# Attention and everything behind it in one stage, with the first output-projection tiles between the last heads' blocks

## What is computed

```python
for i in range(2):
    h = rms_norm(x, g[0])
    # layer 0: 16 heads of 64, each query sees a window of 8 x 16 positions
    # layer 1: 8 heads, softmax(q1 k1) - lam * softmax(q2 k2), an rms norm per head
    m = neighborhood_attention(...) if i == 0 else diff_attention(...)   # ends in o @ w_o
    x = x + rms_norm(m, g[1])
    f = conv_glu_ffn(rms_norm(x, g[2]), ...)          # d_ff 2816, conv of width 3, gelu, gate
    x = x + rms_norm(f, g[3])
    gate = sigmoid(rms_norm(x, g[4]) @ ple_w_gate[i])
    x = x + gate * (p[i] @ ple_w_proj[i])
```

## Time and profile before

| what | value |
|---|---|
| median of three runs | 2300.37 us |
| the profiled execution | 2302.38 us |
| its span, first to last instruction | 2300.6 us |
| PE busy (matmul) | 2188.8 us, 95% |
| PEld busy (weight load) | 1737.0 us, 76% |
| DVE busy | 1282.2 us, 56% |
| ACT busy | 903.2 us, 39% |
| POOL busy | 119.6 us, 5% |
| mean granted TensorE clock | 0.983 |

### The profile page before, as it was taken

How to read it: one execution, slowest core, us unless ns; L and a number is a source line. 1 busy time by engine, 2 the same in 40 slices (tenths; PEclk the granted TensorE clock), 3 DMA queues, 4 the chain that set the end, 5 groups by cost and what they waited for, 6 DMA issues and landing times. The chain is left out here.

```text
span 2300.6 us, 35634 instructions
## 1 busy us (share of the span) xinstructions
PE 2188.8 (95%) x14030; PEld 1737.0 (76%) x14030; DVE 1282.2 (56%) x1653; ACT 903.2 (39%) x1415; POOL 119.6 (5%) x96
## 2 busy tenths in 40 slices
PE   9998999999998999899999998999887799999999
PEld 6786788888876677578888876777767656888887
DVE  6554476563376776457565347685435476433333
ACT  5444432222254565543222244654221354322322
POOL 0000011110000000001111000000313100000000
PEclk9999999999999999999999999999988999999999
DMA  6230323333322221223323331322000011333331
GB/s 245 95 127 23 106 92 100 98 93 101 92 73 91 87 64 45 65 73 110 100 91 100 94 96 56 100 83 64 3 3 3 28 47 50 106 100 93 98 99 65
DMA packets 52933, 187.65 MB, mean 82 GB/s; under 512 B 5840, under 2 KB 6096, under 8 KB 52688
## 3 DMA queue, kind: packets, MB, share of 16 engines
q1 hardware_dynamic: 52528, 185.39, 26.2%
q10 hardware_dynamic: 288, 0.59, 0.1%
HBM read 183.86 MB, written 2.10 MB: 81 GB/s over the span
## 5 line engine op out<-in xcount | busy, mean ns | idle before, releaser
L289 PE MATMUL tail_banks<-tail_r_hi,tail_w_hi 128*128 128x512 f32 x1344 | 529.9, 394 | 7.7 <-DVE tail_r_lo L1678 7.4
L291 PE MATMUL tail_banks<-tail_r_hi,tail_w_lo 128*128 128x512 f32 x1344 | 523.2, 389 | 0.0
L290 PE MATMUL tail_banks<-tail_r_lo,tail_w_hi 128*128 128x512 f32 x1344 | 523.1, 389 | 0.0
L289 PEld LDWEIGHTS tail_banks<-tail_r_hi,tail_w_hi 128*128 128x128 f32 x1344 | 252.3, 188 | 68.2 <-DVE tail_r_lo L1678 7.6
L290 PEld LDWEIGHTS tail_banks<-tail_r_lo,tail_w_hi 128*128 128x128 f32 x1344 | 252.3, 188 | 54.5 <-issue 3.3
L291 PEld LDWEIGHTS tail_banks<-tail_r_hi,tail_w_lo 128*128 128x128 f32 x1344 | 252.2, 188 | 52.9
L274 DVE TENSOR_TENSOR tail_w_lo<-ring,tail_w_hi 128x1024 fp32r<-128x1024 f32 x168 | 241.3, 1438 | 90.8 <-ACT tail_w_hi L268 87.5
L268 ACT ACTIVATE tail_w_hi<-ring 128x1024 fp32r<-128x1024 f32 x168 | 176.7, 1056 | 228.4 <-PE tail_banks L291 225.8
L289 PE MATMUL ff_banks<-ff_r_hi,ff_w_hi 128*128 128x512 f32 x512 | 200.0, 391 | 0.0
L290 PE MATMUL ff_banks<-ff_r_lo,ff_w_hi 128*128 128x512 f32 x512 | 199.2, 389 | 0.0
L291 PE MATMUL ff_banks<-ff_r_hi,ff_w_lo 128*128 128x512 f32 x512 | 199.2, 389 | 0.0
(11 more groups left out here) (527 smaller groups left out, 3486.9 us busy)
## 6 DMA issues: line engine op xcount, KB each, us to landing
ring<-weights SPq DMA_DIRECT2D x315, 512.0 KB, 3.6
na_bias<-window_bias SPq DMA_DIRECT2D x16, 512.0 KB, 5.4
da_rel<-t_rel SPq DMA_DIRECT2D x8, 448.0 KB, 4.3
X<-xT SPq DMA_DIRECT2D x8, 256.0 KB, 5.7
outT<-X SPq DMA_DIRECT2D x8, 256.0 KB, 2.1
const<-consts SPq DMA_DIRECT2D x1, 1312.0 KB, 11.3
tail_pt<-pT SPq DMA_DIRECT2D x2, 512.0 KB, 3.5
kr<-mla_consts SPq DMA_DIRECT2D x1, 512.5 KB, 6.0
```

The source lines that it names most:

```text
L289: pe.matmul(psum, hi, self.r_hi[:, rhs_slot, :], start=start, stop=False)
L290: pe.matmul(psum, hi, self.r_lo[:, rhs_slot, :], start=False, stop=False)
L291: return pe.matmul(psum, lo, self.r_hi[:, rhs_slot, :], start=False, stop=stop)
```

## The change

One stage now holds a layer's attention and its tail (`layer`). `neighborhood` and `differential` no longer open a stage: they return four functions, which the engines' programs of the layer call first. The attention's PSUM tiles are now slices of the layer's 8 banks, its softmax buffer `e` lies in `k.H`. Heads don't go to `k.H`: ScalarE writes each head's tile rounded to a slot of `r_hi`, and VectorE its lo part to `r_lo` (`heads_lo`; in layer 1 over a buffer `heads`, `round_head` and `heads_lo`). `weigh` of layer 0 waits for the lo part of the pair before, not for the copy. In layer 1 `head_out` waits for the lo part of the head two before. The q, k, v products read their right side from slots 2 and 3 and six more, so that heads and inputs don't share slots. Chunks 24 to 27 (the projection's first four) are rounded and split in the last chunks' turns. The projection's tiles 0 to 2 are cut into parts by heads (`wo_part(tile, first, end)`) and stand between the last attention steps; in layer 1 three blocks of tile 3 as well. `keep_busy`, the barrier between the two stages, the rounding of the heads in one go and one load of an activation table on ScalarE are gone. The embedding's load is now the first DMA of a layer.

```diff
 def neighborhood(k, st, sp_, banks, sb, rhs, out):
...
         def weigh(t):
             pe.wait_ge(t_free, turn_of(t, 3))
-            pe.wait_ge(o_out, t) if t else pe.wait_ge(rstd_done, 1)
+            pe.wait_ge(out_split, t) if t else pe.wait_ge(rstd_done, 1)
...
+        def wo_part(tile, first, end):
+            if first == 0:
+                pe.wait_ge(evacuated, N - 2 + tile)
+            if tile == 0:
+                pe.wait_ge(out_split, end)
+            wo(pe, tile, first, end)
+
         chunk((2, last), middle=lambda: scores(last, 1))
         turn_weights(last - 1, 1)
+        wo_part(0, 0, 3)
         turn_values(last - 1)
+        wo_part(1, 0, 3)
         weigh(last - 1)
+        wo_part(0, 3, 6)
         turn_weights(last, 0)
+        wo_part(1, 3, 6)
         turn_weights(last, 1)
+        wo_part(2, 0, 3)
         turn_values(last)
+        wo_part(2, 3, 6)
         weigh(last)
+        for tile in range(FIRST):
+            wo_part(tile, 6, 7)
+        for tile in range(FIRST):
+            wo_part(tile, 7, 8)
...
         def split(c):
-            if c < N:
-                sp_.split_chunk(dve, 0, c)
+            sp_.split_chunk(dve, 0, c)
...
+        def heads_lo(t):
+            dve.wait_ge(o_out, t + 1)
+            dve.tensor_tensor(by_block(sp_.lo(out[t])), o_ps.rearrange("p b (r c) -> p b r c", c=QC),
+                              by_block(sp_.hi(out[t])).bitcast(F32), ALU.subtract).then_inc(out_split, 1)
...
         for t in range(PAIRS):
             evacuate((0, t))
+            if t >= 3:
+                heads_lo(t - 3)
...
         maxima(last)
+        heads_lo(last - 2)
         evacuate((2, last))
         normalise(last)
+        heads_lo(last - 1)
+        heads_lo(last)
...
         last = PAIRS - 1
+        round_ahead((2, last))
         weights_out(last - 1, 1)
...
 def differential(k, st, sp_, banks, sb, rhs, out):
...
+        WO_PARTS = {31: (0, 0, 3), 32: (1, 0, 3), 33: (2, 0, 3), 34: (0, 3, 5), 35: (1, 3, 5), 36: (2, 3, 5)}
         for n in range(NBLK + LAG_O):
...
             if n == NBLK - 1:
                 blocks(done, DT * N)
+            if n in WO_PARTS:
+                wo_part(*WO_PARTS[n])
             if 0 <= n - LAG_T < NBLK:
                 turn_weights(n - LAG_T)
...
+        for tile in range(FIRST):
+            wo_part(tile, 5, 6)
         sum_squares(DA_HEADS - 1)
+        for tile in range(FIRST):
+            wo_part(tile, 6, 7)
+        pe.wait_ge(added, NBLK)
+        wo(pe, FIRST, 0, 3)
+        for tile in range(FIRST):
+            wo_part(tile, 7, 8)
...
+            if n >= 15 and n % TT == 3:
+                heads_lo((n - 15) // TT)
         for h in range((NBLK - 13) // TT + 1, DA_HEADS):
             norm(h)
+            heads_lo(h)
...
             if h >= 2:
                 act.wait_ge(summed, h - 1)
-            act.activation(out[:, h, :], o_ps[:, :], ACT.Copy).then_inc(o_out, 1)
+                act.wait_ge(out_split, h - 1)
+            act.activation(heads[:, h % 2, :], o_ps, ACT.Copy).then_inc(o_out, 1)
...
+        def round_head(h):
+            act.wait_ge(normed, h + 1)
+            act.activation(sp_.hi(out[h]), heads[:, h % 2, :], ACT.Copy).then_inc(out_rounded, 1)
...
+            if n >= 14 and n % TT == 2:
+                round_head((n - 14) // TT)
+        round_head(DA_HEADS - 2)
         rsqrt(DA_HEADS - 1)
+        round_head(DA_HEADS - 1)
...
-def layer_tail(k, layer, m):
+def layer(k, layer):
...
             @block.sync
             def _(sp):
                 sp.dma_start(pt[:, :, :], ...).then_inc(s["pt_loaded"], 16)
-                k.refill(sp, N)
+                att.sync(sp)
+                k.refill(sp, N - WO, WO)
...
-                keep_busy(pe, k, banks[:, 3, :], 4)
-                for j in range(DT):
-                    wo_tile(j)
+                att.tensor(pe, wo)
+                wo(pe, FIRST, 3 if layer else 0, DT)
+                for j in range(FIRST + 1, DT):
+                    wo(pe, j, 0, DT)
...
-                sp_.round_chunk(act, 0, 0)
-                for j in range(DT):
-                    sp_.round_rhs(act, k.H[:, j, :], j)
-                for c in (1, 2, 3):
-                    sp_.round_chunk(act, 0, c)
-                act.preload_act_table_set(LN_EXP)
+                att.scalar(act)
```

More of the change, by code:

```diff
@@ new lines, in neighborhood, with slot, half, by_block @@
+    warm_set = st.sem("warm_set")
+    g0 = k.g
+    def slot(t, h):
+        return 2 * (t % 2) + h
+    def half(h):
+        return slice(64 * h, 64 * h + 64)
+    def by_block(x):
+        return x.rearrange("p (r b c) -> p b r c", b=NB, c=QC)
+    def window(x, b):
+        return x.rearrange("p (r c) -> p r c", c=GRID_W)[:, :, KEY_BASE[b]:KEY_BASE[b] + KC]
+    def turn_of(t, kind):
+        return 3 * t + kind
+    def sync(sp):
+        def load_bias(t):
+            if t >= 2:
+                sp.wait_ge(added, 4 * (t - 1))
+            for h in range(2):
+                sp.dma_start(bias[:, slot(t, h), :, :],
+                             k.dram["window_bias"][2 * t + h].rearrange("p (b j) -> p b j", b=NB)).then_inc(bias_loaded[slot(t, h)], 16)
+        load_start(k, sp)
+        sp.dma_start(k.const[:, :], k.dram["consts"]).then_inc(k.const_loaded, 16)
+        load_bias(0)
+        load_bias(1)
+        for c in range(N):
+            sp.wait_ge(k.chunk_split, g0 + c + 1)
+            sp.dma_start(k.ring[:, (g0 + c) % RING, :], k.dram["weights"][g0 + c + RING, :, :]).then_inc(
+                k.ring_full[(g0 + c) % RING], 16)
+            if c >= 7 and c % 3 == 1:
+                load_bias(c // 3)
@@ L1395, in layer_tail @@
-def layer_tail(k, layer, m):
-    WO, PA, UP, DOWN, PB, GATE = 0, DT, DT + 1, DT + 1 + 2 * FT, DT + 1 + 3 * FT, DT + 2 + 3 * FT
-    N = GATE + DT
-    with Stage(k, f"tail{layer}") as st:
+    qb, kb, vb = (sb(n, [P, 2, S]) for n in ("qb", "kb", "vb"))
+    vt = sb("vt", [P, TT, P])
+    rel = sb("rel", [P, 2, W])
+    lam = sb("lam", [P, 4, 64])
+    lprod = sb("lprod", [P, 2, 64])
+    lsum, lexp, nlam = (sb(n, [P, 2]) for n in ("lsum", "lexp", "nlam"))
+    subg = sb("subg", [P, 1])
+    e = k.H[:, 0:4, :].rearrange("p (n m) s -> p n m s", m=2)
@@ L1511, in down @@
                             pe.wait_ge(s["bank_free"], 2 * FT + o - 3)
[L1512 removed]
+                        mm = sp_.multiply(pe, out(o), DOWN + c, o, two[c % 2], start, stop)
                         if stop and o < DT - 1:
```

1195 lines of the change are left out of this document (579 added, 616 removed).

## The result

The changed kernel takes 2275.95 us (median of four runs, 2272.94 to 2279.24) against 2300.43 us (four runs): ratio 0.9895, 95% interval 0.9878 to 0.9913, a gain of 24.5 us. The forecast was 2269.7, with a range of 2264 to 2276. The result lies at the range's slow edge and 6.3 us above the forecast.

The account below looks back on a forecast made before the run. TensorE's own work plus its holes bounds the kernel. Gains of 16.0 us per layer less 1.3 for the embedding's load make 30.7 us, taken off 2300.37: 2269.7 us, range 2264 to 2276.

Parts of the forecast that it names:

- The ends of attention: From the last chunk or blocks into the projection, in both layers: filled holes on PE gain 16.0 us in each.
- the 1.1 us ahead of the first weigh: Layer 0's end: PE waits 1.1 us at pair 6's weigh for a copy on ScalarE, delayed by rounding.
- the 72 matmuls' stretch: Layer 0, first turn after the last chunk to the projection's 73rd matmul: 42.3 us before, 26.3 forecast.
- The new wait in layer 1: Block 31's scores wait 1.3 us for block 30's bias, delayed by chunk 27's rounding and split.
- The other entries of the sum: Layer 1's end without the new wait: scores, turns, products, sums of squares, 81 matmuls and run entries, 34.3 us.
- The thin margins: Layer 1's end: PE reaches the turns of blocks 29 to 31 only 0.3 to 0.5 us after their maps are mixed.
- The start: The embedding's load, now first, delays the first rounding and first matmul by 1.3 us; bounds 0.5 and 2.
- The clock: Both ends of attention: the clock stays at 1.00, as in the pair loop, despite turns mixed with matmuls.
- hidden at no cost: Lo parts inside both layers' loops: subtractions on DVE and layer 1's roundings are covered and cost 0 us.
- the loops: Layer 0's pair loop and layer 1's block loop: forecast to change by 0 us.
- Rival 1: Thin margins fail or loops pay for new DVE and ACT work: 3 to 8 us, 2273 to 2278; chance 0.17.

Follow-up runs that it names:

- the second set: The unchanged code of the changed kernel measured again, against the kernel before: 2272.15 us against 2302.12, ratio 0.9869.

## Why the prediction was right, and where it failed

*The ends of attention.* Right: 16.1 and 16.7 us for 16.0 and 16.0. The step lengths (turn 0.84, weigh 1.97, nine matmuls 2.0) held, the 1.1 us ahead of the first weigh came as 1.09, and of the 72 matmuls' stretch 26.2 us were measured for 26.3. `heads_lo`, taken as 0.7 us from other rows, took 0.68.

*The new wait in layer 1.* Right in place and cause, 1.67 us for 1.3. Block 30's bias started 3.0 us behind its scores (911.96 to 914.97) where I had 2.5, since ScalarE came to the rounding 0.4 us later than I had it. The other entries of the sum were over-counted by 1.1 us, so that the stretch took 34.9 us for 35.6. The thin margins behind it held: no turn waited for DVE.

*The start.* Right: 0.9 to 1.2 us for 1.3.

*The clock.* Right: 1.00 in both mixed stretches, with 153 matmuls between transposes and weighs. The Trainium skill's page "TensorE: Matmul & The Clock Gate", "Part 4: PE-mode transpose", says that transposes don't count as work for the clock. In the changed kernel nothing fell where they were mixed with matmuls; whether they count by themselves no run here shows. What I had not thought of is that the clock can fall behind the wait that I forecast. It did so in two of the kernels measured, behind 1.87 and 1.88 us, and that cost 1.6 us more; in others it stayed up behind 1.67 and 1.78 us. The 2.19 us wait of the kernel before, behind which it stayed up as well, shows that this is no limit to plan by.

*The step that failed* is "hidden at no cost", and in it the loops. I looked there for work on DVE and ACT and found cover for it, rightly. I took over the 0.227 us of one matmul for all matmuls, also for those that now read another buffer, and so put the loops at nothing. It was 0.2333 for 18 of 24, which cost 2.2 us in layer 0 and 1.4 of the 1.6 us in layer 1. Rival 1 had a price for loops that pay, with the wrong mechanism. The diff showed that the operands of q, k and v move to new buffers, and the row that would have said what this may cost was not in the trace of before, where all operands lay a multiple of 256 bytes from the weights. The Trainium skill's page "SBUF — State Buffer", "Operand start alignment", lets an operand start at any multiple of its element size and says of itself that this is about legality and not speed. The runs here give the speed for TensorE: 227 ns at a distance of a multiple of 256 bytes from the weights, 226 to 237 at any other.

*What remains* of the 6.3 us: the loops took 3.8, and 0.8 at the ends and 0.4 at the start came back, since these terms had been counted too dearly. That leaves 27.8 us of gain at the 82nd matmul, with 24.5 in the medians of the first set and 30.0 in the second. The difference lies behind that point, in stages that the change doesn't touch, 3.3 us one way and 2.3 the other. That the second set came within 0.7 us of the forecast gain is therefore luck. I had given the sum a range as if only its own terms could be off, though the kernel has stages whose clock varies by several us.

## What to carry to other kernels

Where a change gives an operand of TensorE a new buffer, look at its address: against the buffer that the weights are read from, not by itself. A few small buffers allocated ahead of a large one were enough here to lose 3% on each matmul that reads it, and it shows in no list of waits; compare the distances between starts in long runs, grouped by operand.

Filling gaps in TensorE's chain with independent matmuls was worth twice what joining the stages was, and it also kept the clock up. A wait that is left over is worth removing even if it is short: here one of 1.7 to 1.9 us cost 1.8 us in some kernels and 3.5 in others, where the clock fell behind it, and the rows don't say beforehand which it will be.

Compare kernels at fixed points of their work, before the stages that vary most: two executions of the changed kernel agreed there within 0.1 us, where the medians of the two sets lay 3.8 apart. Stretches that begin after a long idle time of TensorE have to be looked at by themselves even so: the first chunk of layer 1 varied by up to 1.2 us.

## What was not expected of the hardware

Matmuls of 512 columns with 128 columns of weights start 227 ns apart in this kernel at the upper clock, if the weights and the right side begin a multiple of 256 bytes apart (0, 256, 512 and 1,024 tried), and up to 10 ns more at 32, 64, 96, 128, 192 or 736 bytes. These are averages over a stage. Single distances in it lie between about 225 and 240 ns, but the average repeats: in five kernels with the same addresses it was 233.0 to 233.6 ns. Moving both by the same 32, 64 or 128 bytes changes nothing. Moving `r_hi` alone by 64 slows the matmuls on `r_lo` too (234 and 235 ns), so it is not the reading of one operand alone. A clash between the reading of the right side and that of the next matmul's weights would look so; that was argued from the pattern and not tested by itself.
